# Retention over spans of queries with two heads side by side, and a norm folded into the guard of the next

## The chip, the cores and the metric

The kernel runs as one launch on one core of a Trainium2 chip. The metric is device time in microseconds (us). Every number below is of that core. The engines are TensorE (PE in rows), VectorE (DVE), ScalarE (ACT), GpSimd (POOL) and SyncE (SP), each with a queue worked off in order.

## The reference

Two transformer blocks in a row, batch 1, width D = 1024, everything in fp32. The first (two diffusion layers with 512 latent and 256 context tokens) is not touched by the change. The second puts 16 meta tokens before the 512 (528 in all) and has two layers of this form:

```python
u = rms_norm(h, norm_mix_pre)
q_r, k_r, v_r, g_r, q_a, k_a, v_a, gate_r, gate_a = split(u @ w_in)
# retention: 8 heads, q and k 64 wide (rotated), v 128 wide
s = (q_r @ k_r.T) * decay          # decay[i, j] = exp(lf * (i - j)) for i >= j, exp(lb * (j - i)) else
o = s @ v_r                        # all 528 keys, forwards and backwards
mu = mean(o); var = mean((o - mu) ** 2)          # over the 128 of a head
y_r = ((o - mu) * rsqrt(var + 1e-6) * silu(g_r)) @ w_ret_o
y_a = window_attention(q_a, k_a, v_a, sink) @ w_att_o
mix = (sigmoid(gate_r) * y_r + sigmoid(gate_a) * y_a) @ w_mix_o
h = h + rms_norm(mix, norm_mix_post)
u = rms_norm(h, norm_ff_pre)
ff = square(relu(u @ w_ff1)) @ w_ff2             # 4096 wide
h = h + rms_norm(ff, norm_ff_post)
```

`rms_norm(x, g)` is `x * rsqrt(mean(x * x) + 1e-6) * g`, over the 1024 features of a token. Only the 512 latent tokens of the last layer are returned.

## The kernel before

Activations are kept transposed: features on the 128 partitions (8 tiles `k` of them), tokens along the free axis. A product with a weight is made exact enough by splitting each operand in two parts of type fp32r (`hi` and `lo`) and adding three products (hi hi, hi lo, lo hi). The weights come by DMA as raw fp32 tiles into three buffers; ScalarE writes `hi` (L1129) and VectorE `lo` (L1698), two weights ahead of the product that needs them (`split_ahead`). `product_T` (L491) is such a product with the weight stationary, `product_N` (L553) the one for values with tokens on the partitions.

Each engine has its own program (`tensor_program`, `scalar_program`, `vector_program`, `pool_program`), all written over the same loops; `tick` and `at` name the events by which they wait for each other. The eight PSUM banks are handed out in turn: `take` gives the bank that has been idle longest and waits until its last reader has freed it, `close` puts it back in line. In some stages work of another stage is laid in between: a `Fill` object is called at fixed points and hands out its share of the pieces of, say, the next projection, measured by a planned cost. All engines use the same plan, so that their queues stay in step.

**Tokens.** `HYBRID` has two spans of tokens, 0 to 272 and 272 to 528, in layer 0. In layer 1 queries need only the 512 latent ones (`LATE`: 16 to 272 and 272 to 528). `ROW_TILES` are the four tiles of 128 tokens and the 16 meta tokens.

**Retention** (`hybrid_layer`, `ret_project`, `ret_units`). Heads are done in four pairs `g`. While a pair is computed, `Fill(8, ...)` lays the projections q, k and v of the next pair (in the last, four gates) between its steps. ScalarE copies v out of the bank (L1477). For k, ScalarE makes padded copies, in which one head of the pair has its 64 rows and the other is zero (`KEY_PAD`, L1510). Then for each head, one after the other:

- scores, keys on the partitions and queries along the free axis: 5 key tiles x 2 spans of queries, on 128 rows (L959);
- VectorE multiplies each out of its bank by the decay strip of the head (L2230). The strip is made from `rel` (distance) by three passes on VectorE (L2209, L2211, L2214) and an exponential on ScalarE (L1500);
- values, with queries on the partitions: 5 query tiles x 5 key tiles, 128 columns each (L970);
- mean and variance per query row by `bn_stats` and `bn_aggr` (L2241, L2245) on VectorE, the power of -1/2 on GpSimd (L2618), normalised rows (L2253), transposed back by TensorE (L983) and copied by ScalarE (L1523).

**The turn from mixing to feed forward** (`turn`, one per engine). The mixed output gets its norm (`mix`): ScalarE squares each tile (L1167), GpSimd adds the squares over the eight tiles (L2413), TensorE adds over partitions (`statistics`, L566), VectorE divides and adds the guard (L1726), GpSimd takes the power of -1/2 (L2423), TensorE spreads it over the partitions (`broadcast`, L576), VectorE scales and adds to the residual (L1776, L1781). Then the same chain is run over the new residual for the norm ahead of the feed forward (`ff`), VectorE scales (L1759), ScalarE writes the `hi` part (L1176), VectorE and GpSimd the `lo` part (L1752, L2429), and the first three products of the feed forward follow (`first_products`, L522). A fence comes next, at which ScalarE, VectorE and GpSimd wait for what all engines have done up to there; behind it the feed forward (`mlp`) begins with ScalarE's relu (L1423). At the end of the feed forward comes its norm (`post`), by the same chain.

## Time and profile before

| | before |
|---|---|
| median of 3 runs | 4081.92 us (4081.37 to 4085.04) |
| the profiled execution, whole | 4079.99 us |
| its span, first to last instruction | 4078.2 us |
| TensorE busy | 3806.4 us (93%) |
| VectorE busy | 1800.4 us (44%) |
| ScalarE busy | 1406.9 us (34%) |
| GpSimd busy | 465.3 us (11%) |
| mean granted clock of TensorE | 0.963 |

Busy time is the union of an engine's instructions; matmuls are pipelined, so the time of one row of them has a tail that lies under the next. On TensorE an fp32 product leaves two records, an fp32r product one. The granted clock is 1.00 at 2.4 GHz and 0.50 at 1.2 GHz. The chain follows the work that ended last back from the end, at each step to what released it. Behind a group of instructions stands the idle time ahead of it and what ended that.

### The profile page before, as it was taken

How to read it: one execution, taken by the hardware profiler on the slowest of the kernel's cores; microseconds unless marked ns; L12 is line 12 of the kernel's file. 1: busy time of each engine (PE TensorE's matmuls, PEld its weight loads, DVE VectorE, ACT ScalarE, POOL GpSimd, SP SyncE). 2: the span in 40 equal slices, each digit the busy share in tenths (PEclk: the TensorE clock that was granted, in tenths of full speed). 3: DMA queues.
4: the chain of work that ended last, by engine and by line, in shares of the span. 5: the costliest groups of instructions: out<-in, count | busy, mean ns of one | idle time of the engine just before them, and what ended most of it. 6: DMA issues, size and time to landing. Idle time of an engine off the chain costs nothing.

```text
span 4078.2 us, 65650 instructions
## 1 busy us (share of the span) xinstructions
PE 3806.4 (93%) x27694; PEld 3402.4 (83%) x27694; DVE 1800.4 (44%) x3333; ACT 1406.9 (34%) x2816; POOL 465.3 (11%) x593
## 2 busy tenths in 40 slices
PE   6988998999999999899989999889997999998998
PEld 5877777888878787788878889889997888988998
DVE  4444465233223555544445553343345556334334
ACT  3444453122122444422321362333232227233322
POOL 1211211000002422100100100110011010011001
PEclk9989999999999999999999999999998999998999
DMA  4022111322231211232210112222221111322222
GB/s 173 29 90 87 56 38 47 104 99 94 94 131 59 70 55 51 78 98 95 102 47 32 53 48 91 76 73 89 90 82 37 42 47 36 97 86 68 94 94 73
DMA packets 88036, 306.12 MB, mean 75 GB/s; under 512 B 9904, under 2 KB 13104, under 8 KB 87616
## 3 DMA queue, kind: packets, MB, share of 16 engines
q1 hardware_dynamic: 84944, 292.72, 21.8%
q0 software_dynamic: 2800, 9.21, 0.7%
q8 instruction: 220, 3.60, 0.4%
q14 instruction: 72, 0.59, 0.1%
HBM read 299.79 MB, written 2.10 MB: 74 GB/s over the span
## 4 chain that ended last, share of the span: by engine, by line
PE 86%; ACT 4%; DVE 4%; POOL 2%; DMA 2%; issue 2%; DVEq 0%; SPq 0%; ACTq 0%; POOLq 0%
PE bank L491 61%; PE bank L553 6%; PE bank L970 3%; PE bank L522 2%; PE bank L959 2%; PE bank L759 2%; POOL scratch L2413 1%; PE bank L798 1%; PE bank L643 1%; PE bank L704 1%; DMA weight_raw<-in_w_mod 1%; PE bank L825 1%; PE bank L850 1%; PE bank L1062 1%; PE bank L923 1%
## 5 line engine op out<-in xcount | busy, mean ns | idle before, releaser
L1698 DVE TENSOR_TENSOR weight_lo<-weight_raw,weight_hi 128x1024 fp32r<-128x1024 f32 (+1 forms) x464 | 555.8, 1201 | 542.0 <-ACT weight_hi L1129 541.9
L491 PE MATMUL bank<-u_hi,weight_hi 128*128 128x256 f32 (+1 forms) x2368 | 684.8, 289 | 8.0 <-DVE u_lo L2353 5.8
L491 PE MATMUL bank<-u_lo,weight_hi 128*128 128x256 f32 (+1 forms) x2368 | 672.8, 284 | 0.0
L491 PE MATMUL bank<-u_hi,weight_lo 128*128 128x256 f32 (+1 forms) x2368 | 671.9, 284 | 0.0
L1129 ACT ACTIVATE weight_hi<-weight_raw 128x1024 fp32r<-128x1024 f32 (+1 forms) x464 | 476.3, 1031 | 511.3 <-PE bank L491 374.5
L491 PE MATMUL bank<-h_hi,weight_hi 128*128 128x512 f32 (+1 forms) x1360 | 498.3, 366 | 30.3 <-DVE h_lo L2082 16.6
L491 PE MATMUL bank<-h_lo,weight_hi 128*128 128x512 f32 (+1 forms) x1360 | 478.6, 352 | 0.0
L491 PE MATMUL bank<-h_hi,weight_lo 128*128 128x512 f32 (+1 forms) x1360 | 478.4, 352 | 0.0
L491 PEld LDWEIGHTS bank<-u_hi,weight_hi 128*128 128x128 f32 x2368 | 448.9, 190 | 35.4 <-issue 25.9
L491 PEld LDWEIGHTS bank<-u_hi,weight_lo 128*128 128x128 f32 x2368 | 449.1, 190 | 0.0
L491 PEld LDWEIGHTS bank<-u_lo,weight_hi 128*128 128x128 f32 x2368 | 447.5, 189 | 0.1
L2413 POOL TENSOR_TENSOR scratch<-scratch 128x256 f32<-128x256 f32 (+2 forms) x154 | 127.5, 830 | 2172.5 <-ACT scratch L1167 2172.4
L491 PEld LDWEIGHTS bank<-h_hi,weight_hi 128*128 128x128 f32 x1360 | 261.2, 192 | 87.4 <-issue 40.5
L491 PE MATMUL bank<-hybrid_hidden_hi,weight_hi 128*128 128x256 f32 (+1 forms) x1024 | 289.6, 283 | 1.1 <-DVE hybrid_hidden_lo L2133 0.8
L491 PE MATMUL bank<-hybrid_hidden_lo,weight_hi 128*128 128x256 f32 (+1 forms) x1024 | 290.4, 284 | 0.0
L491 PEld LDWEIGHTS bank<-h_hi,weight_lo 128*128 128x128 f32 x1360 | 261.0, 192 | 34.6
L491 PE MATMUL bank<-hybrid_hidden_hi,weight_lo 128*128 128x256 f32 (+1 forms) x1024 | 289.4, 283 | 0.0
L491 PEld LDWEIGHTS bank<-h_lo,weight_hi 128*128 128x128 f32 x1360 | 261.8, 192 | 30.1 <-issue 0.5
L491 PE MATMUL bank<-hidden_hi,weight_hi 128*128 128x512 f32 (+1 forms) x792 | 280.4, 354 | 0.0
L491 PE MATMUL bank<-hidden_lo,weight_hi 128*128 128x512 f32 (+1 forms) x792 | 277.2, 350 | 0.0
L491 PE MATMUL bank<-hidden_hi,weight_lo 128*128 128x512 f32 (+1 forms) x792 | 276.8, 350 | 0.0
L2130 DVE TENSOR_TENSOR scratch<-scratch 128x512 f32<-128x512 f32 (+2 forms) x128 | 97.6, 762 | 321.8 <-ACT scratch L1423 321.8
(268 smaller groups left out, 7108.1 us busy)
## 6 DMA issues: line engine op xcount, KB each, us to landing
weight_raw<-in_w_mlp SPq DMA_DIRECT2D x128, 512.0 KB, 3.5
weight_raw<-in_w_ff SPq DMA_DIRECT2D x128, 512.0 KB, 3.5
weight_raw<-in_w_in SPq DMA_DIRECT2D x92, 512.0 KB, 3.5
weight_raw<-in_w_mod SPq DMA_DIRECT2D x80, 512.0 KB, 3.9
weight_raw<-in_a_w_qkv SPq DMA_DIRECT2D x24, 512.0 KB, 4.4
weight_raw<-in_b_w_qkv SPq DMA_DIRECT2D x24, 512.0 KB, 3.6
first_weight<-in_w_mod SPq DMA_DIRECT2D x16, 512.0 KB, 14.5
weight_raw<-in_w_ret_o SPq DMA_DIRECT2D x16, 512.0 KB, 3.5
```

What stands on the lines that cost most here:

```text
L491: m = e.matmul(view[:, 0:hi - lo], a[:, k, :], b[:, k0 + k, lo:hi], start=(k == 0 and i == 0), stop=(k == kt - 1 and i == 2))
L522: m = e.matmul(view[:, 0:hi - lo], a[:, k, :], b[:, k, lo:hi], start=(k == 0 and i == 0), stop=(k == KT - 1 and i == 2))
L553: m = e.matmul(view[:, to:to + 2 * P], b[:, k, lo:lo + P], a[k // 4][:, k % 4, :], start=(k == 0 and i == 0), stop=(k == KT - 1 and i == 2))
L643: m = e.matmul(view[32 * (k % 4):32 * (k % 4) + 32, P * i:P * i + P], csp[:, k, :], w[:, k, :], start=(k < 4), stop=(k >= 4))
L704: m = e.matmul(stat[0][0:n, c:c + 2], sq[:, lo:lo + n], pair_ones, start=True, stop=True)
L759: return e.matmul(view[:, 0:c - a], QK[b][r, hh, P * qt:P * qt + P], QK[b][r, 2 + hh, a:c], start=True, stop=True)
L959: e.matmul(view[0:nk, 0:hi - lo], KEY_PAD[:, hh, k0:k0 + nk], RQ[:, b, lo:hi], start=True, stop=True).then_inc(*tick("pe_score", job))
L970: m = e.matmul(view[0:nq, P * i:P * i + P], SD[0:nk, j, q0:q0 + nq], RV[b][0:nk, j, P * hh:P * hh + P], start=(j == 0), stop=(j == 4))
L1129: e.activation(whi[s % N_SPLIT][:, 0:kt, :], raw[n % N_RAW][:, 0:kt, :], ACT.Copy).then_inc(*tick("act_split", ("hi", n)))
L1698: e.tensor_tensor(wlo[s][:, 0:kt, :], raw[n % N_RAW][:, 0:kt, :], whi[s][:, 0:kt, :].bitcast(F32), ALU.subtract).then_inc(*tick("dve_split ...
L2130: e.tensor_tensor(SCR[:, 2 + j, a:n], SCR[:, j, a:n], SCR[:, j, a:n], ALU.mult).then_inc(*tick("dve_mlp", ("msq", name, q, m)))
L2413: e.tensor_tensor(SCR[:, 5, lo:hi], SCR[:, 5, lo:hi], SCR[:, 4, lo:hi], ALU.add).then_inc(*tick("pool_norm", ("sum", norm, k, span)))
```

## The change

**Retention.** Both heads of a pair are computed together, one span of queries after the other, and `Fill` is called six times per pair instead of eight.

- The padded keys are gone. Both heads' scores run on the 64 partitions on which their rows lie, one pair of products for each key tile and span; VectorE's multiply by the strip stays, with the two heads in turn. There are four strip buffers, and a strip takes two passes on VectorE, not three (a minimum of the two exponents).
- v is centred when it is copied out of its bank, which is now VectorE's work (a sum over the 128 of a head, then one multiply-add). A mean over v's columns taken away ahead of the product takes the mean of the output away too.
- Values have v stationary and the scores moving: 5 products of a whole span for each head. The output comes transposed as it is needed.
- ScalarE copies it to `OR` and squares it; TensorE adds the squares over the partitions (`ret_statistics`), VectorE makes the variance, GpSimd the power, TensorE spreads it (`ret_broadcast`), and VectorE multiplies `OR` by it out of the bank (`ret_normalise`).

**The norm.** With r the inverse root of the `ff` norm, relu and square make the feed forward's output r squared times what it is without r. The `post` norm divides by the root of mean square plus guard, so that r can be left out if the guard 1e-6 becomes 1e-6 times the square of (mean square of the residual + 1e-6). So the turn no longer runs the `ff` chain: `post_norm` writes `lo` right behind its addition (VectorE), `high` reads the residual, and only the statistics of `mix` for span 1 stand among the first products. The squares of the residual are still made, by ScalarE and GpSimd, at the end of the turn; TensorE adds them up in the feed forward's seventh tile, and `guard` makes the row from them.

The core of the diff (of GpSimd's program only its part in the turn, the last lines, is shown; the buffers and the removed lines that can be read in the functions above are cut):

```diff
+                before, free = post or norm, norm and norm[0] == "ff"
                 for product in last:
                     run(product(0))
                 for i, product in enumerate(last):
@@ -599,27 +615,28 @@
                         broadcast(before, 0)
                 for fence in fences:
                     note("pe", "fence", *fence, "pe")
-                if post:
+                if post and not free:
                     statistics(post, 1)
                     broadcast(post, 1)
                 if not jobs:
                     return
-                if post:
+                if post and not free:
                     statistics(norm, 0)
                     broadcast(norm, 0)
                     close("bc", post, 0)
                     close("bc", post, 1)
+                rows = post if free else norm
 
                 def beside(k):
                     if k == 3:
-                        statistics(norm, 1)
+                        statistics(rows, 1)
                     if k == 6:
-                        broadcast(norm, 1)
+                        broadcast(rows, 1)
                 jobs = [(job, weight(key), tok) for job, key, tok in jobs]
                 first_products(jobs, xhi, xlo, norm, 0, beside)
-                close("bc", norm, 0)
+                close("bc", rows, 0)
                 first_products(jobs, xhi, xlo, norm, 1, nothing)
-                close("bc", norm, 1)
+                close("bc", rows, 1)
...
+                        if (name[0], q, m) == ("ffn", 0, 6):
+                            for span in range(2):
+                                statistics(("ff", name[1]), span)
...
+                def ret_scores(g, span):
+                    b = g % 2
+                    lo, hi = tok.spans[span]
+                    for kind in range(2):
+                        e.wait_ge(*at("rr", layer, g, kind))
+                    for j, (k0, nk) in enumerate(ROW_TILES):
+                        views = [take("rs", layer, g, span, j, s) for s in range(2)]
+                        for s in range(2):
+                            r = slice(HD * s, HD * s + HD)
+                            e.matmul(views[s][0:nk, 0:hi - lo], RK[r, b, k0:k0 + nk], RQ[r, b, lo:hi], start=True,
+                                     stop=True).then_inc(
+                                *tick(("pe_scoreu", "pe_scorel")[s], ("rs", layer, g, span, j, s)))
+                        for s in range(2):
+                            close("rs", layer, g, span, j, s)
+                def ret_values(g, span):
+                    lo, hi = tok.spans[span]
+                    e.wait_ge(*at("rvd", layer, g, 2))
+                    for s in range(2):
+                        job = ("ro", layer, g, span, s)
+                        view = take(*job)
+                        e.wait_ge(*at("sd", layer, g, span, s))
+                        for j, (k0, nk) in enumerate(ROW_TILES):
+                            m = e.matmul(view[:, 0:hi - lo], RV[g % 2][0:nk, j, P * s:P * s + P],
+                                         SD[0:nk, s, j, 0:hi - lo], start=(j == 0), stop=(j == 4))
+                        m.then_inc(*tick("pe_value", job))
+                        close(*job)
+                def ret_statistics(g, span):
+                    a = tok.spans[span][0]
+                    view = take("rst", layer, g, span)
+                    for s in range(2):
+                        e.wait_ge(*at("rsq", layer, g, span, s))
+                        for t_, (_, lo, n) in enumerate(tok.rows(span)):
+                            c = 3 * s + t_
+                            m = e.matmul(view[0:n, c:c + 1], RSQ[:, s, lo - a:lo - a + n], ones, start=True, stop=True)
+                    m.then_inc(*tick("pe_row", ("rst", layer, g, span)))
+                    close("rst", layer, g, span)
+                def ret_broadcast(g, span):
+                    a = tok.spans[span][0]
+                    e.wait_ge(*at("rvp", layer, g, span))
+                    for s in range(2):
+                        job = ("rb", layer, g, span, s)
+                        view = take(*job)
+                        for t_, (_, lo, n) in enumerate(tok.rows(span)):
+                            m = e.matmul(view[:, lo - a:lo - a + n],
+                                         spread(ret_var(g, span, 1)[0:n, s, t_:t_ + 1], P), ident[0:n, 0:n], start=True,
+                                         stop=True)
+                        m.then_inc(*tick("pe_row", job))
+                        close(*job)
...
                 def ret_units(g, fill):
-                    b = g % 2
...
+                    ret_scores(g, 0)
+                    if g:
+                        ret_broadcast(g - 1, 1)
+                    fill()
+                    ret_values(g, 0)
+                    ret_scores(g, 1)
+                    fill()
+                    ret_statistics(g, 0)
+                    fill()
+                    ret_broadcast(g, 0)
+                    fill()
+                    ret_values(g, 1)
+                    fill()
+                    ret_statistics(g, 1)
+                    fill()
+                    if g == 3:
+                        ret_broadcast(g, 1)
                     note("pe", "rets", layer, g, "pe")
...
+                if norm[0] == "ff":
+                    e.wait_ge(*at("px", norm_before[norm], k, span))
+                    e.activation(hhi[:, k, lo:hi], x_hyb(k)[:, lo:hi], ACT.Copy,
+                                 scale=vec("ff_pre", KT * norm[1] + k)).then_inc(
+                        *tick("act_norm", ("hh", norm, k, span)))
...
+                if free:
+                    for span in range(2):
+                        for k in range(KT):
+                            square(norm, k, span, x_hyb(k), "px", post, k)
...
+                def ret_out(g, span):
+                    lo, hi = tok.spans[span]
+                    for s in range(2):
+                        job = ("ro", layer, g, span, s)
+                        e.wait_ge(*at(*job))
+                        e.activation(OR[:, 2 * g + s, lo:hi], view_of(*job)[:, 0:hi - lo], ACT.Copy).then_inc(
+                            *tick("act_attn", ("ror", layer, g, span, s)))
+                        e.wait_ge(*at("rst", *ret_before(layer, g, span)))
+                        e.activation(RSQ[:, s, 0:hi - lo], view_of(*job)[:, 0:hi - lo], ACT.Square).then_inc(
+                            *tick("act_attn", ("rsq", layer, g, span, s), ("free", *job)))
...
+                    for span in range(2):
+                        if g < 3:
+                            decay_strip(2 * g + 2 + span)
+                        fill()
+                        ret_out(g, span)
                         fill()
                         fill()
...
+            def guard(layer):
+
+                norm, m = ("ff", layer), None
+                tiles = [row for span in range(2) for row in norm_tokens(norm).rows(span)]
+                for span in range(2):
+                    e.wait_ge(*at("stat", norm, span))
+                    e.wait_ge(*at("rs", ("post", layer - 1), span))
+                    view = view_of("stat", norm, span)
+                    for i, _, n in norm_tokens(norm).rows(span):
+                        m = e.tensor_scalar(RE[0:n, i:i + 1], view[0:n, i:i + 1], 1.0 / D, EPS, ALU.mult, ALU.add)
+                    m.then_inc(*tick("dve_norm", ("re", layer), ("free", "stat", norm, span)))
+                e.wait_ge(*at("re", layer))
+                for i, _, n in tiles:
+                    m = e.scalar_tensor_tensor(out=RE[0:n, i:i + 1], in0=RE[0:n, i:i + 1], scalar=EPS,
+                                               in1=RE[0:n, i:i + 1], op0=ALU.mult, op1=ALU.mult)
+                m.then_inc(*tick("dve_norm", ("guard", layer)))
...
+                def low(k):
+                    e.wait_ge(*at("hh", behind, k, span))
+                    e.scalar_tensor_tensor(
+                        out=U_LO[:, k, lo:hi], in0=x_hyb(k)[:, lo:hi], scalar=vec("ff_pre", KT * norm[1] + k),
+                        in1=U_HI[:, k, lo:hi].bitcast(F32), op0=ALU.mult, op1=ALU.subtract).then_inc(
+                        *tick("dve_norm", ("hl", behind, k, span)))
...
+                def centre_values(g, part, rows, nj):
+                    job = ("rv", layer, g, part)
+                    v = view_of(*job)[0:rows, 0:2 * P * nj].rearrange("p (j c) -> p j c", c=P)
+                    sums = RSUM[0:rows, 0:2 * nj]
+                    e.wait_ge(*at("prod", *job))
+                    for other in OTHERS:
+                        e.wait_ge(*at("rets", layer, g - 2, other))
+                    e.wait_ge(*(at("rvd", layer, g, part - 1) if part else at("rvd", layer, g - 1, 2)))
+                    e.tensor_reduce(sums, v, AX, ALU.add).then_inc(*tick("dve_proj", ("rsum", layer, g, part)))
+                    e.wait_ge(*at("rsum", layer, g, part))
+                    e.scalar_tensor_tensor(
+                        out=RV[g % 2][0:rows, 2 * part:2 * part + nj, :].rearrange("p j (s c) -> p (j s) c", s=2),
+                        in0=sums.unsqueeze(2).to_broadcast([rows, 2 * nj, P]), scalar=-1.0 / P, in1=v, op0=ALU.mult,
+                        op1=ALU.add).then_inc(*tick("dve_proj", ("rvd", layer, g, part), ("free", *job)))
...
-                    e.wait_ge(*at("sd", layer, h - 2))
-                    e.tensor_scalar(E[:, :], rel, 0.0, lf, ALU.max, ALU.mult)
-                    e.wait_ge(*at("dlog", layer, h - 1))
-                    e.tensor_scalar(T2[:, :], rel, 0.0, lb, ALU.min, ALU.mult).then_inc(
+                    for s in range(2):
+                        e.wait_ge(*at("sd", layer, h // 2 - 2, 1, s))
+                    e.tensor_scalar(x, rel, lb, -1.0, ALU.mult, ALU.mult).then_inc(
                         *tick("dve_attn", ("dpart", layer, h)))
                     e.wait_ge(*at("dpart", layer, h))
-                    e.tensor_tensor(E[:, :], E[:, :], T2[:, :], ALU.subtract).then_inc(
+                    e.scalar_tensor_tensor(out=x, in0=rel, scalar=lf, in1=x, op0=ALU.mult, op1=ALU.min).then_inc(
                         *tick("dve_attn", ("dlog", layer, h)))
 
+                def ret_decay(g, span):
+                    lo, hi = tok.spans[span]
+                    for s in range(2):
+                        e.wait_ge(*at("dec", layer, 2 * g + s))
+                        e.wait_ge(*at("ro", *ret_before(layer, g, span), s))
+                    for j, (k0, nk) in enumerate(ROW_TILES):
+                        for s in range(2):
+                            job = ("rs", layer, g, span, j, s)
+                            u = N_LAT - k0
+                            e.wait_ge(*at(*job))
+                            e.tensor_tensor(SD[0:nk, s, j, 0:hi - lo], view_of(*job)[0:nk, 0:hi - lo],
+                                            DEC[(2 * g + s) % 4][0:nk, u + lo:u + hi], ALU.mult).then_inc(
+                                *tick("dve_attn", ("sd", layer, g, span, s), ("free", *job)))
...
+                    ret_decay(g, 0)
+                    if g:
+                        ret_normalise(g - 1, 1)
+                    if g < 3:
+                        decay_strip(2 * g + 2)
+                    fill()
+                    ret_decay(g, 1)
+                    fill()
+                    ret_variance(g, 0)
+                    fill()
+                    ret_normalise(g, 0)
+                    if g < 3:
+                        decay_strip(2 * g + 3)
+                    fill()
+                    fill()
+                    ret_variance(g, 1)
+                    fill()
+                    if g == 3:
+                        ret_normalise(g, 1)
...
+                if norm and norm[0] == "ff":
+                    inverse_rms(post, 1)
+                    for span in range(2):
+                        for k in range(KT):
+                            add_square(norm, k, span)
+                    return
```

## Rows read from the trace of the kernel before

**Rows 1.** the page: its first line, and the chain by engine

```profile
span 4078.2 us, 65650 instructions
PE 86%; ACT 4%; DVE 4%; POOL 2%; DMA 2%; issue 2%; DVEq 0%; SPq 0%; ACTq 0%; POOLq 0%
```

**Rows 2.** windows: busy us (count) of PE, PEld, DVE, ACT, POOL; clock, DMA

```profile
2124.93:2179.75 54.82, 53.44 (x374) 46.82 (x374) 28.15 (x68) 11.22 (x20) 4.90 (x4) 1.00 0.12 39
3173.75:3228.57 54.82, 53.45 (x375) 46.82 (x375) 28.15 (x68) 11.22 (x20) 4.90 (x4) 1.00 0.12 39
2050.30:2056.18 5.88, 5.88 (x28) 5.88 (x28) 2.12 (x2) 0.00 (x0) 0.00 (x0) 0.50 0.77 239
2056.18:2062.00 5.82, 5.82 (x52) 5.82 (x51) 0.00 (x0) 0.60 (x1) 0.00 (x0) 1.00 0.09 32
```

**Rows 3.** timeline of PE in retention: start, us, line, count

```profile
2122.80 0.76 PE L983 MATMUL bank<-shape_constants,ret_rows 128*128 128x128 f32 x5
2124.93 4.82 PE L959 MATMUL bank<-ret_q,ret_keys_padded 128*128 128x272 f32 x20 [1.38 <-ACT ret_keys_padded L1510]
2133.50 7.27 PE L970 MATMUL bank<-ret_v,ret_scores 128*128 128x128 f32 x50
```

**Rows 4.** timeline of PE: pace of fp32 products and loads

```profile
283.52 1.40 PE L704 MATMUL bank<-shape_constants,scratch 128*128 128x2 f32 x12
...
285.82 0.70 PE L759 MATMUL bank<-qk 64*128 64x256 f32 x4
...
2105.09 0.98 PEld L970 LDWEIGHTS bank<-ret_v,ret_scores 128*128 128x128 f32 x8
2105.20 1.05 PE L970 MATMUL bank<-ret_v,ret_scores 128*128 128x128 f32 x8
...
2172.99 1.05 PE L923 MATMUL bank<-ret_q,hybrid_tables 128*128 128x272 f32 x4
2173.88 1.05 PE L923 MATMUL bank<-ret_k,hybrid_tables 128*128 128x272 f32 x4
...
2634.31 1.00 PE L576 MATMUL bank<-shape_constants,row_inverse_rms 16*128 16x16 f32 x6 [0.36 <-POOL row_inverse_rms L2423]
```

**Rows 5.** groups of DVE's instructions, the first four of one pair's window

```profile
L2230 DVE TENSOR_TENSOR ret_scores<-bank,decay 128x272 f32<-128x272 f32 x8 | 3.5, 442 | 5.7 <-PE bank L959 5.5
L2214 DVE TENSOR_TENSOR decay<-decay,decay 128x1040 f32<-128x1040 f32 x2 | 2.5, 1244 | 0.1
L2209 DVE TENSOR_SCALAR decay<-hybrid_tables,log_decay 128x1040 f32<-128x1040 f32 x2 | 1.5, 740 | 0.0
L2169 DVE TENSOR_TENSOR ret_q<-hybrid_tmp 128x528 f32<-128x528 f32 x1 | 0.7, 707 | 0.0
...
L1991 DVE TENSOR_REDUCE small<-bank 128x1 f32<-128x512 f32 x64 | 41.5, 686 | 40.4 <-PE bank L759 39.9
```

**Rows 6.** timeline of ACT in the turn of layer 0

```profile
2644.63 0.43 ACT L1167 ACTIVATE scratch<-residual 128x272 f32<-128x272 f32 x1 [0.93 <-POOL scratch L2413]
2645.99 0.43 ACT L1167 ACTIVATE scratch<-residual 128x272 f32<-128x272 f32 x1 [0.93 <-POOL scratch L2413]
...
2682.09 0.40 ACT L1423 ACTIVATE scratch<-bank 128x272 f32<-128x272 f32 x1 [0.98 <-POOL u_lo L2429]
2683.46 0.39 ACT L1423 ACTIVATE scratch<-bank 128x256 f32<-128x256 f32 x1 [0.97 <-PE bank L522]
```

**Rows 7.** timeline of DVE there

```profile
2638.28 0.48 DVE L1776 SCALAR_TENSOR_TENSOR scratch<-mix_out_T,vectors,bank 128x272 f32<-128x272 f32 x1
...
2639.16 0.49 DVE L1776 SCALAR_TENSOR_TENSOR scratch<-mix_out_T,vectors,bank 128x272 f32<-128x272 f32 x1
```

**Rows 8.** timeline of POOL there

```profile
2645.14 0.76 POOL L2413 TENSOR_TENSOR scratch<-scratch 128x272 f32<-128x272 f32 x1 [0.60 <-ACT scratch L1167]
```

**Rows 9.** timeline of PE there

```profile
2640.88 0.61 PE L566 MATMUL bank<-shape_constants,scratch 128*128 128x1 f32 x4 [2.73 <-POOL scratch L2413]
...
2687.72 0.36 PE L491 MATMUL bank<-u_hi,weight_hi 128*128 128x272 f32 x1 [1.10 <-DVE weight_lo L1698]
```

More of the change, by code:

```diff
@@ L1179, in turn @@
             def turn(post, norm, count, last, splits, hhi):
+                free = norm and norm[0] == "ff"
                 for i in range(count):
@@ L1188, in turn @@
                         for k in range(2):
-                            if post and norm:
+                            if post and norm and not free:
                                 square(norm, k, 0, x_hyb(k), "px", post, k)
@@ L1192, in turn @@
                                 high(norm, k, 0, hhi)
-                if post and norm:
+                if post and norm and not free:
                     for span in range(2):
@@ L1198, in turn @@
                     for span in range(2):
-                        for k in range(0 if span or post else 2, KT):
+                        for k in range(0 if span or post and not free else 2, KT):
                             high(norm, k, span, hhi)
+                if free:
+                    for span in range(2):
+                        for k in range(KT):
+                            square(norm, k, span, x_hyb(k), "px", post, k)
             def first_norm():
@@ L1781, in post_norm @@
                     e.tensor_tensor(x, x, tmp, ALU.add).then_inc(*tick("dve_norm", ("px", norm, k, span)))
+                    if behind and k:
+                        low(k - 1)
                     yield
+                if behind:
+                    low(KT - 1)
             def turn(post, norm, count, last, splits):
[L1786 removed]
+                before, free = post or norm, norm and norm[0] == "ff"
                 for i in range(count):
@@ L1790, in turn @@
                     gain_scale(before)
-                tiles = (post_norm if post else normalise)(before, 0)
+                tiles = post_norm(post, 0, norm if free else None) if post else normalise(norm, 0)
                 for i in range(count):
@@ L1802, in turn @@
                     next(tiles)
-                if post:
+                if post and not free:
                     mean_square(post, 1)
@@ L1820, in turn @@
                 run(tiles)
-                run(normalise(norm, 1))
+                run(post_norm(post, 1, norm) if free else normalise(norm, 1))
             def modulation(layer, m_from, m_to):
```

204 lines of the change are left out of this document (69 added, 135 removed).

## The prediction

> **What bounds the kernel now.** I read the page's shares first, then the chain, then two windows, then the timeline inside them. The chain that ended last runs on TensorE for 86% of the span [rows 1], so what TensorE issues, and the few places where it stands still, set the time. The change touches two places, each of them met twice, once per layer: the retention units, and the turn from the mixing norm to the feed forward.
>
> Retention is a strict period of 54.82 us per pair of heads, the same to 0.01 us in both layers; TensorE is busy for 53.4 of it at the full clock, VectorE for 28, ScalarE for 11 [rows 2]. So it is bound by TensorE's own work. In one period stand two runs of scores of 4.82 us (20 records of TensorE, two per fp32 product), two runs of values of 7.27 us (50 records), and two sets of transposes of 0.76, one followed by a wait of 1.38 for the padded keys [rows 3]. A row's time has a tail of 0.07 that lies under what follows (0.14 for the short ones), so to the next start these are 4.75, 7.20, 0.69 and 2.13. That is 9.5 + 14.4 + 2.8 = 26.7 us; the other 28.1 us are projections of the next pair, which stay.
>
> **Values.** Old: 25 products of 128 columns per head. A run of 8 records with 128 rows takes 1.05 us less its tail, 0.112 apart, but the whole run averages 0.144 [rows 3, 4]; the surplus of 50 x 0.032 = 1.6 us belongs to the five key tiles of 16 rows, some 0.34 each. New: 20 products per pair over 264 columns on average, 40 records. Such an fp32 record costs 0.222 (the rotation: 0.89 us for four of 272 and 256 columns [rows 4]): 8.9 us, plus 4 short tiles x 0.34 = 1.4, so 10.2 in layer 0 and 10.0 in layer 1 (256 columns only). Saved: 4.2 and 4.4. Bounds: 8.9 (the short tiles hide behind the longer streams) and 11.6 (every record 0.29, which is twice 0.144).
>
> The Trainium skill (TensorE: Matmul & The Clock Gate, What overlaps and what doesn't) says that a weight load overlaps a running product only when it goes to another row group. By that rule every record of the new values would show its load too. The rows disagree: eight loads take 0.98 us and the eight products behind them 1.05 in the same stretch, all on the same 128 rows [rows 4]. It is a rival below with a small chance.
>
> **Scores.** Old: 20 products per pair on 128 rows, with half of the key rows zero, 0.475 each. New: the same 20, but two heads side by side on 64 rows each, so 10 passes of two records. Two such products of 256 columns took 0.63 us to the next start (0.70 with the tail), started together [rows 4]; alone they would be 4 x 0.216 = 0.86. A lone pair carries a start of its own. Per span of five pairs I bound it by 10 x 0.222 + 0.1 = 2.3 us (streams only) and 5 x 0.63 = 3.2, and take 2.75, between, since the loads within a run may or may not hide: 5.5 per pair of heads, against 9.5. VectorE's ten multiplies of 0.44 [rows 5] take 4.4 us per span and are slower than this; there are eight banks, so only the fifth pair waits for the first two multiplies, about 1.9 us in, and what follows takes banks that are free by then. Values wait for the last multiply, at about 5.3 us, but one share of projections (28.1 / 6 = 4.7 us) lies between: no wait.
>
> **Statistics and broadcast instead of transposes.** New per pair: 10 one-column products (8 in layer 1), 20 or 16 records at 0.105 (twelve two-column records: 1.40 us with a 0.14 tail [rows 4]): 2.1 or 1.7 us. Then 10 or 8 broadcasts of 128 columns: six records with the 16-row tile 0.76 us, the others 0.105 each [rows 4]: 2 x 0.76 + 8 x 0.105 = 2.4, or 1.7. The transposes and the wait for padded keys go, 2.8. Each step has a share of projections of 4.7 us ahead of it: ScalarE needs 4 x 0.4 = 1.6 us for copy and square (a square is 0.43 [rows 6]), VectorE and GpSimd some 2 us for variance and power, so I cost these waits at nothing; if VectorE came more than 2.7 us late there, the surplus would show.
>
> **What is late next.** Centring of the values moves from ScalarE to VectorE: a reduce of 512 columns (0.69 [rows 5]) and a multiply-add of about the same, 1.3 us per part, queued ahead of the rotation of q and k, which is 3.2 us long (four multiplies like those of the scores at 0.44 and two adds of 0.71 [rows 5]). From the end of part 1 that makes 5.0 us, against 1.6 + 3.0 of TensorE (rotation and part 2): the next scores wait 0.4 us. It takes the place of the 1.38. VectorE's sum per pair: 20 multiplies 8.8, two strips at 0.74 + 1.24 = 4.0 [rows 5] (one pass less than before), centring 3.3, normalising 1.7, splits and rotation 8.0: 26 us, no more than the 28 before.
>
> Per pair: layer 0 5.5 + 10.2 + 2.1 + 2.4 + 0.4 = 20.6, saved 6.1; layer 1 5.4 + 10.0 + 1.7 + 1.7 + 0.4 = 19.2, saved 7.5. Four pairs each: 24.4 + 30.0 = **54.4 us**. At the edge of each layer two decay strips stand on VectorE ahead of the first splits instead of one (+0.6), and the first scores no longer wait for the padded keys (-0.9): -0.6 in all.
>
> **The turn to the feed forward.** Now TensorE stops at 2638.15 (2640.88 less 2.73), and only at 2687.72 does it run freely [rows 9]; in those 50 us two norms are computed in a row. The change takes the second out of the way: products may start as soon as the first norm is added. For that VectorE issues three operations per tile instead of two. Two are 0.88 us apart now (2638.28 to 2639.16 [rows 7]), the third, of the same kind as the first (0.48), adds some 0.42: 1.30. Counted from 2635.35, where the first tile stands, with the split (1.2) and the wait for the row sums after the fourth tile, the first span is done at about 2650, its broadcast at 2651.3, the second span (8 x 1.25) at 2661.3. TensorE has its three first products done by 2665, 21 us sooner than now (1.7 before 2687.72).
>
> But ScalarE's queue is in order: the 16 squares of the dropped norm are not gone, they stand behind the highs and ahead of the first relu, and a fence makes that relu wait for GpSimd's last sum. A square and its sum are one chain of 1.36 us per tile (2644.63 to 2645.99, [rows 6, 8]; 1.31 for 256 columns). Fourteen of these and the two heads are 19.5 us: from 2661.5 to 2681.1. Both relus are then done at 2681.9, against 2683.85 now (the second one at 2683.46 waits for TensorE [rows 6]). **The turn gains 2.0 us, not 21.** And TensorE now stands still for some 20 us there, and starts at the lower clock. After the stall of 8 us at the start of layer 0's retention it ran 28 records in 5.88 us at a granted clock of 0.50, then 52 in 5.82 at 1.00 [rows 2], that is at 1.2 and then 2.4 GHz: 28 x (0.21 - 0.113) = 2.7 us lost, which this turn does not pay now, since it is at the full clock before 2687. Added too: ten one-column products in the seventh tile, 0.9 us. So +2.7 + 0.9 - 2.0 = +1.6 per layer, **+3.2 us** (bounds -5 and +8: pitch of the tiles 1.2 to 1.4 us, restart paid or not). The guard on VectorE, ten small operations, lies beside products. No transfer is added, taken away or reordered by either part, so SyncE's queue is left as it is.
>
> **Sum.** 4079.99 (the execution profiled, 1.8 us over its span) - 54.4 - 0.6 + 3.2 = 4028.2. The median of the runs shown is 1.9 us higher: **4030 us**.
>
> **The rivals.** (A) Scores stay at the pace of the evictions: the run of a span takes 4.8 us as now. For it: VectorE is the slower of the two (4.4 us against 2.75), and banks are taken in turn. Against: only the fifth pair needs a bank twice. It gives back 2.1 x 16 = 33: 4063. The Trainium skill (TensorEngine Tiling (Array Packing), PSUM Bottleneck) warns of just this: tiling speeds up TensorE, not the emptying of its banks. (B) Every weight load shows: 60 records per pair x 0.105 = 6.3, less the 2.3 that I count already (short tiles, starts of scores), 32 us: 4062. Against it the paces above. (C) The turn pays in full, because the first relus get ahead of the squares: 2 x 19 us less: 3992. Against it the order in the queue and the fence. (D) Slower: VectorE's queue becomes the bound, since each of the 16 spans has a chain square, statistics, variance, power, broadcast, in order behind ten multiplies. It begins to cost when VectorE is 2.7 us late, and eats the whole gain when it is 6 us late in every span (16 x 3.3 = 52); at 6.5 us: 4030 + 16 x 3.8 = 4091. Against it VectorE's 26 us in a period of 48. (E) The short tiles hide and the loads of the scores too: another 18 us, 4012; that is the low side of my own case.
>
> **How the numbers follow.** Forecast with its own bounds 0.78, A 0.09, B 0.04, C 0.04, D 0.02; the last 0.03 for something else that costs. A measurement tells a change from none beyond 0.2%, 8 us. Faster: all but D and the last, 0.95; same 0.02; slower 0.03. The range goes down to 4006 (all terms good) and up to 4058 (scores near A, or half a microsecond more wait per span and a turn of +8).
>
> **What would show it.** In retention: a period of 47 to 49 us; in it two runs of values of about 5.1 us, two of scores of 2.3 to 3.2, and no rows of ret_keys_padded. In the turn: first products before 2640 in old time, TensorE idle for about 20 us before the fourth tile, a row of sixteen squares 1.3 us apart ahead of the first relu, and the low clock behind it. Wrong would be: scores near 4.8 us (A), values above 5.8 (B), a relu ahead of the squares (C), TensorE waiting for variance or power in each span (D).

## The result and the profile after

The changed kernel takes **4031.25 us** (median of 4, 4029.61 to 4032.93) against 4081.64; the ratio is 0.9872 (0.986 to 0.9885). The forecast was 4030. The profiled execution has a span of 4029.6 us, against 4078.2 [rows 1]. The sum came out almost exactly, and that is partly luck: two of its terms were off by 7 and by 3 us in opposite directions.

To see it, I cut both traces at five events of each layer that both kernels have, as microseconds between them (worked out from TensorE's start times; a layer's retention begins here with its first product for v, the window with its first rotation, the mixing with the second record of the first product with w_ret_o, and the feed forward with the first product over hidden tiles):

```
                          start  retention  window,  mix and  feed     retention  window,  mix and  feed
                                 layer 0    branches turn     forward  layer 1    branches turn     forward
before                  2050.30   239.87     135.54   291.34   382.83   238.15     119.93   282.02   338.21
changed                 2052.26   220.01     134.00   290.08   381.63   210.26     119.95   283.07   338.34
changed again (run 10)  2055.22   219.97     134.00   290.11   381.60   210.39     119.98   283.01   338.28
```

Behind the first 2050 us every stage of the changed kernel repeats to 0.15 us between two chips, so one profile is enough for it. What differs from run to run lies in the first stage, which the change does not touch, and the 2 us that the changed kernel is behind there say nothing of it. The rest: retention -19.9 and -27.9, the turns with their mixing -1.3 and +1.1, together -0.2; the window stage of layer 0 -1.5 and the feed forward of layer 0 -1.2.

The windows of one pair, layer 0 and layer 1, of the changed kernel (columns as in [rows 2]):

```profile
2120.13:2170.41 50.28, 48.74 (x344) 42.35 (x345) 24.84 (x48) 10.07 (x18) 5.23 (x4) 1.00 0.13 43
3143.07:3191.30 48.23, 46.69 (x336) 41.16 (x337) 24.59 (x47) 10.02 (x18) 5.23 (x4) 1.00 0.14 45
```

A pair took 54.82. Now it is 50.3 and 48.2 us, of which TensorE stands still for 1.54 in each. Where, its timeline says (start, us, line, count), with the lines that answer to [rows 3]:

```profile
2120.13 2.67 PE L979 MATMUL bank<-ret_q,ret_k 64*128 64x272 f32 x20 [1.55 <-DVE ret_k L2263]
2122.73 1.16 PE L1016 MATMUL bank<-shape_constants,ret_variance 128*128 128x128 f32 x8
2128.84 5.33 PE L993 MATMUL bank<-ret_scores,ret_v 128*128 128x272 f32 x20
2134.10 2.68 PE L979 MATMUL bank<-ret_q,ret_k 64*128 64x256 f32 x20
2141.33 1.41 PE L1005 MATMUL bank<-shape_constants,ret_squares 128*16 128x1 f32 x12
2147.74 1.99 PE L1016 MATMUL bank<-shape_constants,ret_variance 16*128 16x16 f32 x12
```

Scores 2.67 instead of 4.82, a pair's values 5.33 and some 5 instead of 7.27 twice, no padded keys. But each pair's first scores wait for `ret_k`. VectorE's and GpSimd's timelines ahead of such a wait:

```profile
2164.17 0.17 DVE L2350 TENSOR_SCALAR ret_variance<-bank 128x4 f32<-128x4 f32 x1 [10.15 <-PE bank L1005]
2164.25 0.69 DVE L2279 TENSOR_REDUCE ret_value_sums<-bank 128x4 f32<-128x512 f32 x1
2164.98 0.69 DVE L2281 SCALAR_TENSOR_TENSOR ret_v<-ret_value_sums,bank 128x512 f32<-128x512 f32 x1
2165.58 0.77 DVE L2259 TENSOR_TENSOR hybrid_tmp<-bank,hybrid_tables 128x272 f32<-128x272 f32 x2
2167.14 1.75 DVE L2263 TENSOR_TENSOR ret_q<-hybrid_tmp 128x528 f32<-128x528 f32 x1 [0.79 <-POOL hybrid_tmp L2735]
```

```profile
2164.41 1.32 POOL L2750 TENSOR_TENSOR ret_variance<-ret_variance,minus_half 128x6 f32<-128x6 f32 x1 [20.02 <-DVE ret_variance L2350]
2165.70 1.33 POOL L2735 TENSOR_TENSOR hybrid_tmp<-ret_q,hybrid_tables 128x528 f32<-128x528 f32 x1
2166.99 1.33 POOL L2735 TENSOR_TENSOR hybrid_tmp<-ret_k,hybrid_tables 128x528 f32<-128x528 f32 x1
```

GpSimd has been idle for 20 us, and then does its power and the two multiplies for the rotation in a row. VectorE's addition waits 0.79 us for the first, and takes 1.75 us beside the second, where it takes 0.71 [rows 5] otherwise. Centring (2164.25 to 2165.58) ends earlier than GpSimd does.

In the turn of layer 0 ScalarE's timeline shows the squares of the new residual, and the first relu behind them (of the answers to [rows 6], four):

```profile
2641.41 0.73 ACT L1220 ACTIVATE scratch<-residual 128x272 f32<-128x272 f32 x2
2643.02 0.43 ACT L1220 ACTIVATE scratch<-residual 128x272 f32<-128x272 f32 x1 [0.88 <-POOL scratch L2537]
...
2657.74 0.42 ACT L1220 ACTIVATE scratch<-residual 128x256 f32<-128x256 f32 x1 [0.83 <-POOL scratch L2537]
2659.13 0.67 ACT L1487 ACTIVATE scratch<-bank 128x272 f32<-128x272 f32 x2 [0.97 <-POOL scratch L2537]
```

and TensorE's shows how long it stood there, where 1.10 us stand in [rows 9]:

```profile
2663.67 0.57 PE L506 MATMUL bank<-u_hi,weight_hi 128*128 128x272 f32 x1 [17.66 <-DVE weight_lo L1755]
```

The row names the weight's split, since ScalarE and VectorE reach it only behind the relus. Two windows behind it show the restart, 21 records at the low clock:

```profile
2663.67:2668.51 4.84, 4.84 (x21) 4.84 (x22) 3.18 (x5) 2.98 (x6) 0.00 (x0) 0.51 0.42 132
2668.51:2672.00 3.49, 3.49 (x32) 3.49 (x31) 1.77 (x2) 1.12 (x3) 0.00 (x0) 1.00 0.43 140
```

One trap: the page's chain of waits gives TensorE 41% now, where it was 86% [rows 1]. The list behind it begins only at 2052.26 us, so the two shares can't be compared.

### The profile page after: what moved, and what is told of

Read it like the earlier page. It is cut to its first block and busy times, and to the rows that moved or that the text cites. A ratio compares the mean times of both kernels' runs of the same rounds, so it can differ in the third digit from the quotient of the medians.

```text
span 4029.6 us, 64955 instructions
## 1 busy us (share of the span) xinstructions
PE 3762.4 (93%) x27404; PEld 3359.8 (83%) x27404; DVE 1758.9 (44%) x3158; ACT 1400.9 (35%) x2808; POOL 449.8 (11%) x571
```

## The experiments

**1 and 2: each part alone.** The two parts of the diff share no line but a buffer's; each was put on the kernel before by itself.

```diff
# run 1, on the kernel before: turn, post_norm, high, guard, mean_square, inverse_before and the statistics in the seventh tile
+                if free:
+                    for span in range(2):
+                        for k in range(KT):
+                            square(norm, k, span, x_hyb(k), "px", post, k)
...
# run 2, on the kernel before: ret_units and what it calls, centre_values, decay_strip, the buffers
+                    ret_scores(g, 0)
...
```

> The kernel before with the norm part of the change alone (old retention). Theory (squares stay in ScalarE's queue ahead of the first relu): the turns together cost about nothing, -2 to +4 us against before, so 4080 to 4086. TensorE stands idle for 17 to 19 us ahead of the fourth tile's product in each turn and runs its first 20 or so records behind it at half clock. Rival (the turn was worth its planned gain and retention fell short by as much): -8 us or more. Rival (the turn costs by its cold restart): +8 us or more.

> The kernel before with the retention part alone (old turn and norms). Theory: the whole gain is here, -47 to -52 us, so 4030 to 4035; periods of 50.3 us in layer 0 and 48.2 in layer 1, against 54.82. Rival: the two parts help or hinder each other (the clock, the two norms' buffers), then this run and the norm part alone don't add up to the -50 of both, by more than 4 us.

The norm alone: 4080.16 us against 4082.6 on that chip, ratio 0.9998 (0.9989 to 1.0006): no change. Ahead of the fourth tile TensorE is idle for 17.68 and 17.30 us, as expected. Retention alone: 4034.26, ratio 0.9885 (0.9871 to 0.9899). -2.4 and -48.3 us add up to -50.7; the whole change was -50.4. Stage by stage the retention's 220.01 and 210.76 us are within 0.5 us of the changed kernel's 220.01 and 210.26. The parts don't meet, and the gain is all retention's.

**3: scores head after head.** In `ret_scores` and VectorE's `ret_decay` the loops change places:

```diff
-                    for j, (k0, nk) in enumerate(ROW_TILES):
-                        for s in range(2):
+                    for s in range(2):
+                        for j, (k0, nk) in enumerate(ROW_TILES):
```

> The changed kernel, with the scores of a span issued head after head (five key tiles of one, then five of the other) and VectorE's multiplies in the same order; the same products, banks and bytes. Theory (the speed of the scores comes from two heads running side by side on their own halves of the rows): a run of scores takes 20 x 0.22 = 4.4 us instead of 2.60, and the 16 runs cost 16 x 1.8 = 29 us at most; since the wait for the rotation ahead of the next scores doesn't take up any of it, 4055 to 4062. Rival (it comes from the smaller operands or from better order, not from running side by side): 2.6 to 2.8 us as now, 4031.

Measured: 4098.93 us, ratio to before 1.0046 (1.0031 to 1.006). The order of the scores alone turns the gain into a loss: +67.7 us where I expected at most 29. A run of scores at the full clock takes 4.91 us, where I expected 4.4 (2.60 with both heads side by side; the old ones of [rows 3] take 4.75 to the next start). So the rival is out, and my price of the order was too low. But TensorE's timeline has this for the first run of a pair:

```profile
2127.73 9.22 PE L979 MATMUL bank<-ret_q,ret_k 64*128 64x272 f32 x20 [1.59 <-DVE ret_k L2262]
```

and the windows there say why (granted clock: third number from the end):

```profile
2124.00:2127.73 3.73, 2.14 (x19) 1.96 (x18) 3.27 (x5) 0.00 (x0) 1.60 (x2) 1.00 0.00 0
2127.73:2130.00 2.27, 2.27 (x7) 1.74 (x8) 1.47 (x4) 0.00 (x0) 0.00 (x0) 0.66 0.00 0
2130.00:2133.00 3.00, 3.00 (x7) 1.18 (x6) 1.31 (x3) 0.00 (x0) 0.00 (x0) 0.50 0.00 0
2136.90:2140.00 3.10, 3.10 (x15) 3.10 (x15) 1.78 (x4) 0.00 (x0) 0.00 (x0) 0.50 0.00 0
2142.00:2145.40 3.40, 3.40 (x30) 3.40 (x30) 1.82 (x2) 2.78 (x4) 0.00 (x0) 0.99 0.00 0
```

The clock goes to 1.2 GHz in the scores and stays there into the projections. All six runs that stand behind a wait for the rotation take 7.0 to 9.4 us; the ten others take 4.9 to 5.2. So 16 x 2.3 = 37 us are the order, and some 31, what is left of the 67.7, are clock.

**4: the squares beside the feed forward.** The 16 squares leave the turn and are handed out one by one in `mlp`; GpSimd adds behind its fence; statistics and guard move to the second quarter.

```diff
-                if free:
-                    for span in range(2):
-                        for k in range(KT):
-                            square(norm, k, span, x_hyb(k), "px", post, k)
...
-                mlp(("ffn", layer), HYB_HID, tok, tok, f"w_ff1_{layer}", f"w_ff2_{layer}", finish)
+                def squares():
+                    for span in range(2):
+                        for k in range(KT):
+                            square(("ff", layer), k, span, x_hyb(k), "px", ("mix", layer), k)
+                            yield
+                mlp(("ffn", layer), HYB_HID, tok, tok, f"w_ff1_{layer}", f"w_ff2_{layer}", finish, squares())
...
-                        if (name[0], q, m) == ("ffn", 0, 6):
+                        if (name[0], q, m) == ("ffn", 1, 4):
```

> The changed kernel, with the 16 squares of the residual and GpSimd's sums taken out of the turn and laid one by one beside the feed forward's products (statistics and guard in its second quarter). Theory (the squares ahead of the first relu are what holds TensorE): the idle time of 17.9 us goes down to 2 to 5 us, and the 21 records at half clock behind it (2.3 us) are mostly gone: 14 to 18 us per turn, 28 to 36 in all, 3995 to 4003. Rival (something else is late next in the turn, such as the weight's split or the fence): less than 10 us per turn, 4011 or more. Rival (the squares slow the relus in the feed forward, which is bound by TensorE but close to ScalarE): TensorE waits for the hidden tiles and part of it is given back.

Measured: 3994.04 us, ratio 0.9788 (0.9775 to 0.9802), 37 us under the changed kernel and 1 us under the expected range. The stages of mixing and turn take 270.16 and 263.52 us, 19.9 and 19.6 less; the feed forwards take 2.0 and 0.8 more. Some 1.0 and 0.8 of that are the row sums' one-column products, which the edit moves out of the one stage into the other. TensorE's waits for hidden tiles are what they were (0.8 us, in layer 1 alone), so the last rival is out. TensorE's row ahead of the fourth tile:

```profile
2647.40 0.36 PE L506 MATMUL bank<-u_hi,weight_hi 128*128 128x272 f32 x1 [1.10 <-DVE weight_lo L1757]
```

and the window behind it, at the full clock from the first record:

```profile
2647.40:2651.00 3.60, 3.60 (x29) 3.60 (x30) 2.65 (x4) 2.15 (x4) 0.00 (x0) 1.00 0.44 146
```

So the squares with GpSimd's sums, and nothing else in the turn, held TensorE for these 17 us.

**5 to 7: who is late in the rotation.**

```diff
# run 5, GpSimd's ret_units
                         fill()
                         fill()
+                        if span:
+                            fill()
                         e.wait_ge(*at("rvar", layer, g, span))
...
-                        fill()
+                        if not span:
+                            fill()
# run 6, VectorE's ret_project; run 7 has both
-                        centre_values(g, part, rows, nj)
                         if part == 1:
                             for kind, dst in ((0, RQ), (1, RK)):
                                 rotate(dst[:, b, :], ("rrot", layer, g, kind), tab(1), kind,
...
+                        centre_values(g, part, rows, nj)
```

> The changed kernel; GpSimd does its two multiplies for the next pair's rotation ahead of the power of the second span instead of behind it. Theory (the wait of 1.6 us ahead of a pair's first scores, six times, is GpSimd's: power, then the multiplies for q and k, 1.3 us each, and the addition of q that runs 1.75 us beside them): each wait goes down by 1.2 to 1.6 us, 4021 to 4024. Rival (my term of the prediction: VectorE's centring of 1.3 us ahead of the rotation is what is late): at most 0.4 us each, 4029 or more, since the order on VectorE is left as it is.

> The changed kernel; VectorE rotates q and k ahead of the centring of the second part of v, GpSimd's order left as it is. Theory (GpSimd's multiplies are late): VectorE's products are done sooner but the additions still wait for GpSimd, so the wait shrinks by 0.3 to 1 us each, 4025 to 4029. Rival (the centring is what is late): the whole 1.3 us each, 4023.

> Both orders of the two runs before together. Theory: no wait is left, 6 x 1.6 = 9.7 us against the changed kernel, 4021 to 4022; with GpSimd's alone giving the same within 1 us. Rival (both are needed, each alone gives little): this one gains at least 4 us more than either alone.

GpSimd first: 4024.96 us, ratio 0.9863 (0.9848 to 0.9878). VectorE first: 4039.19, 0.9898 (0.9884 to 0.9913), slower than the changed kernel. Both: 4021.77, 0.9855 (0.984 to 0.987). Run 5's GpSimd and its windows of a pair:

```profile
2149.49 1.32 POOL L2735 TENSOR_TENSOR hybrid_tmp<-ret_q,hybrid_tables 128x528 f32<-128x528 f32 x1
2150.76 1.34 POOL L2735 TENSOR_TENSOR hybrid_tmp<-ret_k,hybrid_tables 128x528 f32<-128x528 f32 x1
2169.54 1.32 POOL L2752 TENSOR_TENSOR ret_variance<-ret_variance,minus_half 128x6 f32<-128x6 f32 x1 [17.44 <-DVE ret_variance L2350]
```

```profile
2125.16:2173.85 48.69, 48.69 (x346) 42.16 (x344) 24.28 (x47) 10.07 (x18) 5.23 (x4) 1.00 0.14 44
3144.82:3191.50 46.68, 46.68 (x337) 41.06 (x336) 23.96 (x46) 10.02 (x18) 5.21 (x4) 1.00 0.14 46
```

Counted from the pair's first scores the multiplies run some 21 us earlier (2149.49 - 2125.16 = 24.3 us in, against 2165.70 - 2120.13 = 45.6), the wait is gone, VectorE's addition for q is back at 0.71 us, and TensorE is busy for all of the 48.69 us; each period is 1.6 us shorter. The retention stages take 4.8 and 4.9 us less, 9.7 together, as the theory says. The median is 1 us above the range that I expected: it moved by 6.3, since 1.6 of it stands again in the next stage of layer 0 (135.58 against 134.00), and the first stage is slow in these runs. My expectation for run 6 missed (4025 to 4029), its rival's too. The wait did not shrink at all:

```profile
2169.79 0.73 PE L979 MATMUL bank<-ret_q,ret_k 64*128 64x272 f32 x4 [1.53 <-DVE ret_k L2263]
2171.06 2.38 PE L979 MATMUL bank<-ret_q,ret_k 64*128 64x272 f32 x16 [0.55 <-DVE ret_v L2281]
```

and the centring, now behind the rotation, keeps a bank that the scores need (0.55 <- `ret_v`) and stands ahead of VectorE's ten multiplies. In three of the six places the clock falls too: these runs take 4.46, 4.95 and 4.51 us at a mean clock of 0.75, 0.66 and 0.71, the three others 3.5 to 3.6 us at 1.00. Run 7 without the wait shows none of it, and gives no more than run 5: the periods are 48.7 and 46.8, and though its median is 3.2 us lower, the retention stages together are 0.9 us longer and the intervals of the two ratios overlap. In the profiled executions the difference lies in the first stage.

**8: scores head after head, without the wait.** The loops of run 3 on the kernel of run 7.

```diff
-                    for j, (k0, nk) in enumerate(ROW_TILES):
-                        for s in range(2):
+                    for s in range(2):
+                        for j, (k0, nk) in enumerate(ROW_TILES):
```

> The kernel of the run before with the scores again head after head. In the earlier run with scores in this order the runs took 4.91 us at the full clock, and the first of a pair 7.0 to 9.4 us at a granted clock of 0.50 behind each of the six waits of 1.87 us. Theory (the wait and the thin run of scores behind it together bring the clock down; head after head costs 4.91 - 2.60 = 2.3 us by itself): without the wait the clock stays at 1.00, all 16 runs take 4.9 us and the kernel comes 16 x 2.3 = 37 us behind the run before, some 4058. Rival (the thin run alone brings the clock down): runs of 7 us and more stay, 4080 or more.

Measured: 4060.45 us, 38.7 above run 7, where 37 were expected. All 16 runs take 4.91 to 5.17 us at a granted clock of 1.00. (The 1.87 us of the expectation run from the start of the record before; TensorE's idle time in run 3 was 1.59.) So the clock's fall in run 3 needs the wait of 1.6 us and the thin run behind it; the thin run alone keeps the full clock.

**9 and 10: both improvements, and the changed kernel again.** Run 9 is the edits of 4 and 5 together.

```diff
# on the changed kernel: run 4's edit, and in GpSimd's ret_units
+                        if span:
+                            fill()
...
```

> The changed kernel with both edits that helped: the squares beside the feed forward's products, and GpSimd's multiplies for the rotation ahead of its power. Theory (they touch different stages, each limited by its own wait): the gains add up, 37 us for the squares and 6 x 1.6 = 9.7 for the order on GpSimd, 3984 to 3988, with periods of 48.7 and 46.7 us and no idle time over 2 us ahead of the fourth tile. Rival: the clock or the weights take part of it back, 3992 or more.

> The changed kernel once more beside it on the same chip: 4029 to 4033. What the stages that no edit touches differ by between two profiled executions of one program shows here; I expect up to 2 us, of which the 1.96 us that the changed kernel was behind before the first retention would be one.

Run 9: **3988.28 us**, ratio to before 0.9768 (0.9754 to 0.9783), the best of all. Run 10 beside it: 4034.74, 0.9882 (0.9865 to 0.9898), a little above what I expected. On another chip the same kernel took 4031.25, so medians from different chips that are 3 or 4 us apart say nothing by themselves; there I go by the stages. One pair of run 9, without idle time:

```profile
2124.27:2172.96 48.69, 48.69 (x346) 42.16 (x345) 24.29 (x47) 10.07 (x18) 5.23 (x4) 1.00 0.13 44
```

The gain over the changed kernel beside it is 46.5 us, against 47 expected.

## Why the prediction was right, and where it was off

**Values: right.** Forecast 10.2 and 10.0 us per pair; measured to the next start 5.26 + 4.99 = 10.25 and 2 x 4.99 = 9.98. In a run of 20 records over 272 columns most are 0.229 us apart, and seven at or next to the two products with 16 rows 0.32 to 0.33. That is 0.7 us more in a run, 0.34 for each short tile, just the price that I took from [rows 3, 4]. The weight loads of the full tiles stay hidden. Rival B is out.

**Scores: right, a little high.** Forecast 2.75 per span, measured 2.47 to 2.61. The two heads' records start 0.007 to 0.036 us apart, and the next pair some 0.2 later. Runs 3 and 8 show that this is what side by side buys. The evictions don't set the pace (rival A, 4.8): VectorE's ten multiplies take 3.56 us (4.4 forecast) and end after TensorE has left, and nothing waits for them. The Trainium skill's warning (TensorEngine Tiling (Array Packing), PSUM Bottleneck), that tiling does not speed up the emptying of banks, did not come to bear with eight banks and ten products.

**Statistics and broadcast: right.** 2.08 against 2.1 us, 2.66 against 2.4, in layer 1 1.62 against 1.7 and 1.72 against 1.7.

**What is late next: the step that failed.** I put the wait ahead of a pair's first scores at 0.4 us, from VectorE's centring in front of the rotation. It is 1.55 us of idle time, and it is GpSimd's: its multiplies for q and k stand behind a power that hangs on the second span's statistics. I had named GpSimd's power for its own wait, but never asked what else is in that queue. Runs 5 and 6 settle it: GpSimd's order alone takes the wait away, VectorE's alone does not. With GpSimd's order changed, the centring in front of the rotation costs no wait at all, so my own term was wrong too (its 5.0 us hold 0.5 that no row gives: the named parts are 1.3 + 3.2).

Both retentions together fell short by 7.2 us (-19.9 and -27.9 against -24.4 - 30.0 - 0.6). The wait is 6.1 of it: six times 1.55 us, against eight times 0.4. The other 1.1 is what is left of several small terms, summed over TensorE's records in both stages: scores -2.5, one-column sums -0.4, broadcasts +0.9, values +0.1; the projections between the units, which I took as unchanged, +1.7; and +1.4 at the edges of the layers: the first old wait of a layer is 0.99 us and not 1.38, the sum's -0.9 takes it off a second time (it is in the four pairs already), and the +0.6 for the strips did not show.

**The turn: right in its mechanism, a little dear.** Counted from the start of TensorE's last product of mixing (2617.76; 2637.87 in the trace of before), the squares start after 23.65 us, where the forecast had 23.6. They take 17.7 us instead of 19.5, at a pitch of 1.31 and 1.25 us instead of 1.36 and 1.31. From there to the fourth tile it is 45.9 us against 49.85, and 45.6 against 48.0 in layer 1: -3.9 and -2.4, where I had -2.0. The restart at half clock costs 21 x (0.230 - 0.118) = 2.3 us instead of 2.7. With the one-column products (1.05 and 0.8) these terms give about zero, and the table -0.2, instead of +3.2. Rival C, the turn paid in full, was 3992; run 4, which lets the relus get ahead, is 3994.

**The sum.** 4028.2 + 7.2 (retention) - 3.4 (turns) - 1.5 (the stage behind retention in layer 0) - 1.1 (the feed forwards) + 2.0 (the first stage, not the change's) = 4031.4, which is the profiled execution (span 4029.6 and 1.8 around it). That execution stood at the median, so the 1.9 us that the forecast added for the median came to nothing: for the execution it was 3.2 us too low, and only the last step brought it within 1.3. The 1.5 us behind retention stay open: the stage of before and after has the same gaps to 0.01 us, only a slightly closer pace of its records, and run 5 takes it back.

**Rival D** (VectorE too late in every span) is out as a case: VectorE is busy for 24.8 of 50.3 us. Run 6 shows that it is near all the same, once something long stands between the rotation and the multiplies.

## What to carry to other kernels

When a step is moved, walk the queue of every engine that takes part in it, also of the one that is 11% busy: GpSimd's two multiplies could run 21 us earlier and stood behind a wait. Work that is no longer on the path must be moved out of the queue of what is, or nothing is gained: the folded norm was worth nothing that run 1 could measure where it was put, and 37 us when its squares went beside the feed forward. And a forecast that hits the total should still be cut into stages, since here a miss of 7 us hid behind others; and the terms inside a stage too, since in it a wait of 9.3 us hid behind scores that were cheaper than forecast.

## What the runs showed of the hardware

- A wait of 1.6 us on TensorE costs nothing more when two heads' scores side by side follow at once (granted clock 1.00 in six of six places of the changed kernel). When the same products follow one at a time, the clock falls to 0.50 for 7 to 14 us, about 5 us of time each (six of six, run 3). That was nearly half of run 3's loss, and run 8, without the wait, has none of it. Side by side is no guarantee: in run 6 a second gap of 0.55 us lies inside these scores, and the clock fell in three of six places. And one at a time is not enough to bring it down: the old scores ran so on 128 rows behind waits of 1.38 us, at 1.00 (six of six). The Trainium skill (TensorE: Matmul & The Clock Gate, What's actually happening) tells of a gate that halves the array's clock; the two levels agree. Which level a thin stretch gets is from these runs alone.
- Products on the 64 rows of one head alone are not cheaper than on 128: 4.91 us for ten of 256 columns (runs 3 and 8) against 4.75 with padded keys. Side by side on both halves they take 2.60.
- VectorE's addition of 528 columns takes 0.71 us alone and 1.75 beside a GpSimd multiply of the same size that began before it. In all twelve such places (the changed kernel and run 6) it ended 0.56 us after the multiply; one that lay beside it for only 0.82 us took 1.39. So the addition got little done until the multiply was over, and did not just run slower. The multiply kept its 1.33 us.
